# A hybrid decoder layer: step 0's seven products in the order in which their token blocks come, and late token rows at the end of each step

## The reference

```python
u = rms_norm(hid, norm_pre_w)                       # (2048, 1024)
proj = einsum('bsd,de->bse', u, w_in)               # q, k, v, gate, z, conv inputs x/B/C, dt
attn = mixture_of_dilations(q, k, v) * silu(g)
y = gated_group_rms_norm(ssd_chunked(silu(conv(xbc)), softplus(dt), ...), z)
out = einsum('bse,ed->bsd', concat(attn, y), w_out)
return hid + rms_norm(out, norm_post_w)
```

## Time and profile before

| | |
|---|---|
| median of 3 runs | 2194.87 us (2192.63 to 2195.62) |
| the profiled execution | 2193.86 us, span 2192.1 us |
| busy: TensorE, DVE, ACT, POOL | 2131.7, 1374.5, 1039.6, 1443.0 us |

### The profile page before, as it was taken

The page is one execution under the profiler, slowest core; times in us unless marked ns, Lnnn a source line. Parts: engine busy times, 40 slices in busy tenths (PEclk is TensorE's granted clock), DMA queues, the critical chain, the costliest instruction groups (busy, mean ns, idle before and its releaser), DMA issues.

```text
span 2192.1 us, 34748 instructions
## 1 busy us (share of the span) xinstructions
PE 2131.7 (97%) x12009; PEld 1824.1 (83%) x12009; DVE 1374.5 (63%) x2581; ACT 1039.6 (47%) x2412; POOL 1443.0 (66%) x877
## 2 busy tenths in 40 slices
PE   6999999999999999999999999999997999999998
PEld 4778888888888887888889999999996788888877
DVE  7656666444556665363477777777777866766662
ACT  5334444343433443344357777777775622332231
POOL 5778888777678987777845564655642555655552
PEclk9999999999999999999999999999998899999999
DMA  4552333333623333343375656556547444434431
GB/s 152 198 182 88 111 109 116 115 97 122 224 94 99 96 125 106 109 122 97 115 168 127 155 135 145 120 146 155 135 110 250 153 140 145 139 125 135 135 104 58
DMA packets 261564, 288.23 MB, mean 131 GB/s; under 512 B 78516, under 2 KB 229232, under 8 KB 253328
## 3 DMA queue, kind: packets, MB, share of 16 engines
q1 hardware_dynamic: 260384, 278.68, 43.1%
q0 software_dynamic: 1008, 7.34, 0.8%
HBM read 195.80 MB, written 81.53 MB: 127 GB/s over the span
## 4 chain that ended last, share of the span: by engine, by line
PE 87%; DVE 4%; issue 3%; ACT 3%; DMA 2%; POOL 1%; SPq 0%; DVEq 0%; POOLq 0%; ACTq 0%
PE mm L1124 14%; PE mm L1126 14%; PE mm L1125 14%; PE ps_o L1885 9%; PE ps_t L1872 5%; PE ps_out L2481 5%; PE ps_out L2482 5%; PE ps_out L2488 5%; PE ps_s L1864 4%; PE ps_s L1865 3%; PE ps_y L2523 2%; PE turn L1226 2%; PE ps_state L2513 1%; PE ps_y L2504 1%; DMA tok_tile<-in_x_dram 1%
## 5 line engine op out<-in xcount | busy, mean ns | idle before, releaser
L1124 PE MATMUL mm<-b_hi,w_hi 128*128 128x512 f32 x1456 | 572.3, 393 | 8.3 <-DVE fm L902 6.5
L1126 PE MATMUL mm<-b_hi,w_lo 128*128 128x512 f32 x1456 | 567.9, 390 | 0.0
L1125 PE MATMUL mm<-b_lo,w_hi 128*128 128x512 f32 x1456 | 567.4, 390 | 0.0
L603 POOL TENSOR_TENSOR w_lo<-w_raw,w_hi 128x512 fp32r<-128x512 f32 x208 | 301.3, 1456 | 79.7 <-ACT w_hi L676 72.0
L1124 PEld LDWEIGHTS mm<-b_hi,w_hi 128*128 128x128 f32 x1456 | 273.9, 188 | 66.3 <-issue 10.4
L1126 PEld LDWEIGHTS mm<-b_hi,w_lo 128*128 128x128 f32 x1456 | 273.8, 188 | 57.6
L1125 PEld LDWEIGHTS mm<-b_lo,w_hi 128*128 128x128 f32 x1456 | 274.1, 188 | 55.6
L676 ACT ACTIVATE w_hi<-w_raw 128x512 fp32r<-128x512 f32 x208 | 130.8, 630 | 261.3 <-PE mm L1126 240.8
L1872 PE MATMUL ps_t<-ident_b,probs 128*128 128x128 f32 x1136 | 213.5, 278 | 6.3 <-ACT probs L1797 5.0
L902 DVE SCALAR_TENSOR_TENSOR fm<-mm,u 128x512 f32<-128x512 f32 x120 | 92.3, 769 | 181.9 <-PE mm L1126 181.7
L2481 PE MATMUL ps_out<-wo_hi,mix_hi 128*128 128x512 f32 x480 | 193.9, 404 | 1.3 <-ACT mix_hi L2374 1.3
(11 more groups left out here) (266 smaller groups left out, 4460.9 us busy)
## 6 DMA issues: line engine op xcount, KB each, us to landing
w_raw<-in_w_in_dram SPq DMA_DIRECT2D x52, 1024.0 KB, 5.3
feat<-fm SPq DMA_DIRECT2D x56, 512.0 KB, 5.0
tok<-tok_tile SPq DMA_DIRECT2D x52, 512.0 KB, 3.5
raw_q<-feat SPq DMA_DIRECT2D x32, 512.0 KB, 5.8
raw_k<-feat SPq DMA_DIRECT2D x32, 512.0 KB, 6.4
cum_b<-cum_scratch SPq DMA_DIRECT2D x16, 1024.0 KB, 7.5
cls_nat<-cls_out SPq DMA_DIRECT2D x64, 132.0 KB, 2.7
v_cls<-tok SPq DMA_DIRECT2D x64, 128.0 KB, 4.0
```

What stands on the lines that cost most here:

```text
L603: pool.tensor_tensor(wl[o][:, :, :], source(o, n), wh[o][:, :, :].bitcast(F32), ALU.subtract)\
L1124: pe.matmul(bank, w_hi[:, k, :], bh[o][:, k, :], start=(opens and k == 0), stop=False)
L1125: pe.matmul(bank, w_hi[:, k, :], bl[o][:, k, :], start=False, stop=False)
L1126: last = pe.matmul(bank, w_lo[:, k, :], bh[o][:, k, :], start=False, stop=(closes and k == KH - 1))
```

## The change

Step 0's products are computed in the order A11, A12, S1, S4, S3, S2, A22, each as soon as its token operand is there, between the transposes of the pieces; the pieces come by kind (B22 and T1 lane by lane, then all T3, all T2, all T4). The weight parts of step 0 are made in the order A11, A12, S1, S2, S4, S3, A22. T2 is written over B22's rows, squares go to other rooms, dt's early product is stored in two halves, earlier. The weights of step 1 are loaded before the first late rows and no longer after all pieces. The squares of late rows stand further back in ACT's list (`late_squares`), and their normalise and sums behind the last read of the step on DVE (`late_rows`).

```diff
+FIRST_ORDER = (A11, A12, S1, S4, S3, S2, A22)
+FIRST_MADE = (A11, A12, S1, S2, S4, S3, A22)
...
-        START_PARTS += [(o, j) for j in range(LANES) for o in (B22, T1, T3, T2, T4)]
+        START_PARTS += [(o, j) for j in range(LANES) for o in (B22, T1)]
+        START_PARTS += [(o, j) for o in (T3, T2, T4) for j in range(LANES)]
...
         def sync(sp):
...
+            for tb in range(2):
+                sp.wait_ge(dt_read, tb + 1)
+                sp.dma_start(dram["dt"][0:2 * SSM_HEADS, block_cols(tb)], dt_early_out[tb]).then_inc(dt_stored, 16)
+            sp.wait_ge(u_turned, PART_AT[T2, LANES - 1] + 1)
+            sp.wait_ge(sums_dve, 2 * LANES)
+            load_w(1)
             for i in range(HT, HT + 2):
-                sp.wait_ge(u_turned, GROUP_AT + 5 * (i - HT + 1))
                 load_x(i)
-            sp.wait_ge(u_turned, START)
-            load_w(1)
 
             for s in steps:
...
-                sp.wait_ge(lo_made, PRODUCTS * n + 6)
+                sp.wait_ge(lo_made, PRODUCTS * n + (6 if n else PRODUCTS))
...
         def gpsimd(pool):
...
+            low(A11, 0)
+            low(A12, 0)
+            token_sum(T1, 0)
+            sum_one(0)
+            token_sum(T1, 1)
+            low(S1, 0)
+            token_sum(T1, 2)
             pool.wait_ge(dt_hi_made, 1)
             pool.tensor_tensor(dt_w[:, :, SSM_HEADS:2 * SSM_HEADS], dt_raw[:, :, :],
                                dt_w[:, :, 0:SSM_HEADS].bitcast(F32), ALU.subtract).then_inc(dt_lo_made, 1)
+            sum_two(0)
+            token_sum(T1, 3)
+            for j in range(LANES):
+                token_sum(T3, j)
+            low(S2, 0)
             last_sum(0)
+            low(S4, 0)
+            sum_three(0)
+            low(S3, 0)
+            low(A22, 0)
+            low(A11, 1)
...
         def scalar(act):
...
             for s in steps:
                 n = s.n
-                if n in PREP:
-                    for half in range(2):
-                        square(HT + 2 * PREP[n] + half)
+                if n == 0:
+                    high(0, 1)
+                    late_squares(0)
...
                 high(2, n + 1)
                 reload(n, 2)
+                if n:
+                    late_squares(n)
...
         def vector(dve):
...
+            dve.wait_ge(act_read, 1)
+            read(steps[0], A12, put(steps[0], 0, 0), c1[:, :])
+            for i, then in enumerate((T2, T4, None)):
+                for j in range(LANES):
+                    if then is not None:
+                        token_sum(then, j)
+                    r = SUMS_AT + LANES * i + j
+                    token_low(r, START_PARTS[r])
+            dve.wait_ge(dt_stored, 32)
+            read(steps[0], S2, u2[:, :], c1[:, :])
...
-                if n in PREP:
-                    for half in range(2):
-                        normalise(HT + 2 * PREP[n] + half)
+                if n == 0:
+                    dve.wait_ge(u_turned, START)
+                    late_rows(0)
+                    continue
...
                 read(s, S2, u2[:, :], c1[:, :])
-                if n in PREP:
-                    late_sums(PREP[n])
...
                 read(s, S4, put(s, 0, 1), u2[:, :])
                 reload(n, 6)
+                if n in PREP:
+                    late_rows(n)
...
         def tensor(pe):
...
             for j in range(LANES):
-                for r in range(GROUP_AT + 5 * j, GROUP_AT + 5 * j + 5):
+                for r in range(GROUP_AT + 2 * j, GROUP_AT + 2 * j + 2):
                     early_rows(r)
-                    if r == GROUP_AT:
-                        multiply(steps[0], 0)
                 if j == 0:
+                    multiply(steps[0], A11)
+                elif j == 1:
+                    multiply(steps[0], A12)
+                elif j == 2:
                     pe.wait_ge(dt_lo_made, 1)
                     dt_part(dt_banks[0], 0, B11, opens=True)
...
+            for i in range(3):
+                for j in range(LANES):
+                    early_rows(SUMS_AT + LANES * i + j)
+                    if i == 0 and j == 0:
+                        pe.wait_ge(act_read, 1)
+                        dt_part(dt_banks[1], 0, B11, opens=True)
+                    elif i == 0 and j == 1:
+                        multiply(steps[0], S1)
+                    elif i == 0 and j == 3:
+                        pe.wait_ge(u_lo_made, 4 * LANES)
+                        dt_part(dt_banks[1], 0, T1)
+                        dt_part(dt_banks[1], 1, B22, closes=True).then_inc(dt_product, 1)
+                    elif i == 1 and j == 1:
+                        multiply(steps[0], S4)
+                    elif i == 2 and j == 0:
+                        multiply(steps[0], S3)
+                    elif i == 2 and j == 2:
+                        multiply(steps[0], S2)
+            multiply(steps[0], A22)
```

More of the change, by code:

```diff
@@ L320, in project @@
         START_PARTS = [part for j in range(LANES) for part in ((B11, j), (B21, j))]
-        START_PARTS += [(o, j) for j in range(LANES) for o in (B22, T1, T3, T2, T4)]
+        START_PARTS += [(o, j) for j in range(LANES) for o in (B22, T1)]
+        START_PARTS += [(o, j) for o in (T3, T2, T4) for j in range(LANES)]
+        PART_AT = {part: r for r, part in enumerate(START_PARTS)}
         GROUP_AT = 2 * LANES
+        SUMS_AT = 4 * LANES
+        POOL_SUMS = {part: i + 1 for i, part in enumerate([(o, j) for o in (T1, T3) for j in range(LANES)])}
+        DVE_SUMS = {part: i + 1 for i, part in enumerate([(o, j) for o in (T2, T4) for j in range(LANES)])}
         LATE_PARTS = [(o, j) for o in range(PRODUCTS) for j in range(LANES)]
+        SUM_AT = ({S1: 1, S2: 2, S4: 3, S3: 4}, {S1: 1, S2: 2, S3: 3, S4: 4})
+        PARTS_LOW = {A11: 2 * LANES, A12: 2 * LANES, S1: 4 * LANES, S4: 4 * LANES, S3: 5 * LANES, S2: 6 * LANES, A22: START}
         COLUMN = {B11: 0, B21: 1, B22: 2, T1: 3, T2: 4, T3: 5, T4: 6}
@@ L616, in gpsimd, with token_sum @@
-            sums(0)
-            low(0, 0)
-            token_sums(0)
+            def token_sum(o, j):
+                if o == T1:
+                    pool.wait_ge(normed, j + LANES + 1)
+                    pool.wait_ge(u_turned, PART_AT[B11, j] + 1)
+                    pool.tensor_tensor(u_tok[j][:, 0:BANK], x_room(j + LANES)[:, 0:BANK], u_tok[j][:, 0:BANK],
+                                       ALU.subtract).then_inc(sums_pool, 1)
+                else:
+                    pool.wait_ge(sums_pool, POOL_SUMS[T1, j])
+                    pool.tensor_tensor(x_room(j + LANES)[:, 0:BANK], x_room(j + LANES)[:, BANK:HALF],
+                                       x_room(j + LANES)[:, 0:BANK], ALU.subtract).then_inc(sums_pool, 1)
@@ L684, in square, with late_squares @@
                                scale=1.0 / D_MODEL).then_inc(rooted, 1)
+            def late_squares(n):
+                if n in PREP:
+                    for half in range(2):
+                        square(HT + 2 * PREP[n] + half)
             def token_high(r, part):
@@ L747, in reload, with read_dt_early @@
                         token_high(START + op * LANES + j, (op, j))
[L749 to L753, removed]
+            def read_dt_early(tb):
+                act.wait_ge(dt_product, tb + 1)
+                act.activation(dt_early_out[tb], dt_banks[tb][0:2 * SSM_HEADS, :], ACT.Copy).then_inc(dt_read, 1)
             def read_dt_late():
@@ L894, in late_sums, with late_rows @@
                 dve.tensor_tensor(t4, u21, t2, ALU.subtract).then_inc(sums_late, 1)
+            def late_rows(n):
+                for half in range(2):
+                    normalise(HT + 2 * PREP[n] + half)
+                late_sums(PREP[n])
             def read(s, o, out, more):
-                dve.wait_ge(product, PRODUCTS * s.n + o + 1)
+                dve.wait_ge(product, product_at(o, s.n))
                 seen = bank(s, o)[:, :]
@@ L1030, in vector @@
             for j in range(LANES):
-                token_sums(j)
                 if j < 2:
                     normalise(j + 6)
-                for r in range(GROUP_AT + 5 * j, GROUP_AT + 5 * j + 5):
+                for r in range(GROUP_AT + 2 * j, GROUP_AT + 2 * j + 2):
                     token_low(r, START_PARTS[r])
+            dve.wait_ge(act_read, 1)
[8 more added lines that the diff above has]
+            read(steps[0], S2, u2[:, :], c1[:, :])
+            dve.wait_ge(dve_read, 2)
+            read(steps[0], S3, u3[:, :], u2[:, :])
+            dve.wait_ge(dve_read, 3)
+            read(steps[0], S1, put(steps[0], 1, 1), u3[:, :])
+            read_fifth(steps[0])
+            read(steps[0], A22, put(steps[0], 1, 0), u3[:, :])
+            dve.wait_ge(dve_read, 5)
+            read(steps[0], S4, put(steps[0], 0, 1), u2[:, :])
             dve.wait_ge(taps_turned, 1)
@@ L1253, in tensor @@
                 n = s.n
-                for o in range(PRODUCTS):
-                    if n or o:
-                        multiply(s, o)
```

(2 more changed lines are left out.)

176 lines of the change are left out of this document (85 added, 91 removed).

## The result

The changed kernel takes 2240.16 us (median of 4 runs, 2238.71 to 2242.72) where the kernel before takes 2195.0: a ratio of 1.0209, 95% interval 1.0191 to 1.0227. The forecast was 2237. The profiled execution has a span of 2237.0 us against 2192.1, 44.9 more.

A forecast was written before the change was run, and what follows sets the result against it. TensorE was taken as nearly full, its waits set by a late-rows ring; the change's new ring of 35.1 us a step makes step 4's S4 read 43 us late: 2193.9 + 43 = 2237 us, range 2208 to 2249.

The forecast's parts named there:

- the ring: Steps 1 to 3: late sums wait for S4's read, S4 for A12's read, that for a store behind the previous late sums; 35.1 us.
- end of sums to the store's issue: SP's queue: from the end of late sums to the issue of the feat store, 7.9 us, bounds 7.3 and 9.0.
- landing: DMA: from the feat store's issue until both halves have landed, 10.0 us.
- read to S4: From DVE's A12 read until TensorE starts the step's last product, 0.8 us.
- S4 until its read, with half clock: TensorE's last product until DVE reads it, 3.1 us, plus 2.4 for twelve matmuls at half clock after the wait.
- late rows: DVE, after S4's read: two normalises and four sums, partly beside POOL, 10.2 us, bounds 5.3 and 10.9.
- The waits of 10 to 12 us and of some 4 us: Signs: TensorE waits before the last product of steps 1 to 3 (10 to 12 us) and in step 4 (some 4).
- Step 0: First step, new product order: A11 starts at 26, the step ends at 67 us instead of 72.2, bounds 64 and 72.2.
- Step 4: Conv step: DVE waits at its head for stored rows, landed at 192.2; S4 read at 199.0 against 155.94, 43 us late.
- Blocking in full: Rival: DVE and POOL block each other wholly, late rows 13.0 instead of 10.2 us; 2248 us; chance 0.15, with no step 0 gain.
- POOL out of the way: Rival: the ring binds without POOL's company or a falling clock, 27.8 us a step, 2210 us; chance 0.22.
- Faster: Rival: the previous step's store lands before A12 is to be read, so the three waits go; 2183 us; chance 0.05.

The follow-up runs named there:

- e2_rows_only: The kernel before with only the late rows' squares, normalise and sums moved as in the change, step 0 as before: 2244.06 us, ratio 1.0229.
- e1_store_first: The changed kernel, with SP storing step n's tile to feat ahead of its late rows (n = 0 to 3): 2198.24 us, ratio 1.0018.
- e5_pool_holds: The changed kernel, with POOL starting the weight sums of steps 2 to 5 only after the late sums of steps 0 to 3: 2224.88 us, ratio 1.0147.
- e8_gate_late: e1_store_first with DVE's wait for the stored rows in step 4 moved from the step's head to behind the read of S2: 2192.94 us, ratio 1.0001.
- e7_step4: e8_gate_late plus the split wait for row loads and the last group's sums stored ahead of its rows: 2184.52 us, ratio 0.9959.
- e6_before_split: The kernel before, with row loads waiting only for the two stores out of their own rooms: 2188.3 us, ratio 0.9975.
- e4_fill: The changed kernel with 54 idle matmuls on TensorE in front of S4 of steps 1, 2 and 3: 2239.2 us, ratio 1.0205.
- e3_rows_back: The changed kernel with the late rows of steps 1 to 3, squares included, back in their old place: 2205.93 us, ratio 1.0053.

## Why the prediction was right

**What binds.** Right: the lost time is in steps 1 to 4. In steps 1 to 3 it is the wait before S4, released by a read that waits for the `feat` store; in step 4 it is the wait before A22, for the landing of the last rows. `e2_rows_only` shows that the move makes the ring, `e1_store_first` that the store's place in SP's queue closes it.

**The terms of a turn.** The forecast was 35.1 us; the turns between the ends of late sums (79.38, 115.72, 151.02, 185.89) were 36.3, 35.3 and 34.9. Term by term, forecast against the three turns:

- end of sums to the store's issue: 7.9; 7.27, 7.27, 7.26. The 9.0 of the mean was a turn with an instruction fetch among its stores; the changed kernel had none there.
- landing: 10.0; 10.6, 10.0, 10.2 until the read starts.
- read to S4: 0.8; 0.84 each time.
- S4 until its read, with half clock: 5.5; 5.57, 5.11, 4.50. The clock came back within the product in the later turns (granted 0.50 from 98 to 104 us, 0.65 from 133.8 to 140, 0.73 from 169.2 to 175).
- S4's read: 0.7; 0.61 each time.
- late rows: 10.2; 11.5 each time. This term was mis-sized: its upper bound of 10.9 was too low too. POOL was at work all the time in the stretch that the bound came from as well, but there DVE's read of S2 stood between the normalises and the sums, and the first sum behind it was short: 1.18 us, where it takes 1.66 after the change. That, with 0.1 in the normalises, is the difference. POOL's company costs 5.0 us (`e5_pool_holds`), about the 4.9 that the forecast assumed.

The first sum before and after the change:

```profile
62.48 1.18 DVE L889 TENSOR_TENSOR conv_in<-tok_tile 128x512 f32<-128x512 f32 x1
```
```profile
108.94 1.66 DVE L937 TENSOR_TENSOR conv_in<-tok_tile 128x512 f32<-128x512 f32 x1
```

The errors nearly cancel: S4 of steps 1 to 3 is read at 103.61, 138.92 and 173.78, forecast 103.4, 138.5 and 173.6. The mechanism was foreseen; that the reads agree to 0.4 us is luck, since the late rows were 1.3 us longer than forecast, and the issue of the store and the lost clock shorter. The waits of 10 to 12 us and of some 4 us that the prediction gave as signs do not follow from its own terms: a turn of 35.1 less 19.1 of products and 2.4 of lost clock leaves 13.6, and step 4 some 6, which is what came.

**Step 0.** A11 starts at 26.26 (forecast 26), the wait before A22 is 2.10 (1.9), the step ends at 66.2 (67). The 2.4 for a first product at half clock were some 1.3: the first half of A11's matmuls came every 0.43 us or slower, the rest every 0.23. The 1.40 us for POOL's low part in step 1 are hidden behind the 13 us, as costed, but the late weight load is hardly their cause: POOL starts on step 1's weights at 62.88, when it gets ScalarE's high part of A11, and that stood behind the last token piece on ScalarE until 62.0 and waited only 0.17 us more for the load.

**Step 4.** The late sums ended at 185.89 (forecast 184.5), the landing took 6.57 us (7.65), so A22 started at 193.46 (193.2): two errors that cancel. The forecast left the lost clock of this step out: behind 6.18 us of waiting the granted clock is 0.53 from 193.4 to 200.0, and S4 is read at 202.14 instead of 199.0.

```profile
192.46 0.07 DVE L1125 MEMSET conv_in<- 128x3 f32 x2 [6.57 <-DMA rows<-conv_in]
...
202.14 0.69 DVE L956 SCALAR_TENSOR_TENSOR conv_in<-mm,u 128x512 f32<-128x512 f32 x1 [2.50 <-PE mm L1195]
```

Of these 3.1 us the profiled execution shows 1.8 at its end (2238.71 us against the 2236.9 of the sum); the other 1.3 are won back behind step 4, and no row here says where.

**The rivals.** Blocking in full (2248) priced late rows at 13.0; they took 11.5, between the forecast and this rival. POOL out of the way did not come by itself; made to happen, it gives 2225 with the clock still falling. Faster needed the store to leave earlier: with that edit, the later wait of `e8_gate_late` and the two edits of `e7_step4` the change does win, so this rival named the right place.

## What to carry to other kernels

Before work is moved behind a wait, look up what that wait is for and what has hidden it: here a store that had landed just in time, by estimate some 3.5 us before its reader was free (issue and landing against the read the earlier trace rows), became 17 us of waiting when the reader was free early. A queue in program order ties unrelated things together, so a store whose data are ready should stand ahead of one that waits. And where steps run at the pace of a ring of transfers, shortening one link (here a semaphore that counted four stores where two were meant) can gain more than moving the work along the ring: it gained 4.6 us here (`e6_before_split`), where the change lost 45.

## What was not expected of the hardware

**Stores beside an instruction fetch.** Stores of late rows among which an instruction fetch fell landed later. The ten traces have 40 such groups of stores. In seven the DMA view shows a packet on q8 before the end of the stores, and the two `conv_in` stores landed 5.0 to 5.6 us after issue (5.4 in the kernel before, at 90 us; 5.4 and 5.5 with `e4_fill`; 5.0 in `e5_pool_holds`, whose issues were further apart). In the others it was 4.0 to 4.5, and 3.1 in the one group of `e7_step4` that has another order. The end is a tail of 21 to 41 GB/s in the first stretch of `e4_fill`, where the full part moved about 400; a sixteenth of that, one of the 16 DMA engines of the page, would be 25. That one engine is held up by the fetch fits this, but no run was made that moves a fetch, so the cause stays open. So the ring of the kernel before has turns of two lengths: from the end of the late sums to the issue of the store it took 9.0 us in one turn and 7.3 in two.

**The clock behind one and the same wait.** In the seven traces with the new step 0 that were compared, TensorE's work up to A22 of step 0 is the same, and it waits 2.1 us there in each. The granted clock from 64 to 68 us is 1.00 in four of them (the change, `e3_rows_back`, `e4_fill`, `e8_gate_late`) and 0.57 to 0.60 in three (`e1_store_first`, `e5_pool_holds`, `e7_step4`); step 0's last reads start at 66.1 to 66.5 us in the four and at 68.5 to 68.8 in the three. So the length of a wait does not tell by itself whether the clock falls, and single traces of such kernels can differ by some 2 us for it. What decides it no run shows.
